# Sixteen modulation rows spread over fourteen weight blocks instead of eight, and the compression's matrices fetched at the end of the first phase

## The chip, the cores and the metric

The kernel is one program on one core of a Trainium2 chip. The metric is the device time of one execution in microseconds (us); lower is better. The engines are PE (TensorE), DVE (VectorE), ACT (ScalarE), POOL (GpSimd) and SP (SyncE, which only issues DMAs here). PE's clock is granted in two levels, 1.2 and 2.4 GHz; the profile gives it as a share of the higher one.

## The reference: what is computed

Two transformer-like blocks run one after the other on an activation of 256 tokens by 2048 features. Only the first matters here. Cut to its core:

```
mod = silu(c) @ ada_w + ada_b                      # 6 vectors of 2048: sh1, sc1, g1, sh2, sc2, g2
h = rmsnorm(x) * norm1_g * (1 + sc1) + sh1
z = h @ w_in                                       # q, kc, vc, ks, vs, kw, vw, gates, lx, ly, ga, gb
k_cmp = gelu(blocks(kc + pos_k) @ w1_k) @ w2_k     # compression of 32 tokens, stride 16: 15 keys in 4 groups
v_cmp = gelu(blocks(vc + pos_v) @ w1_v) @ w2_v
o_a = compressed + selected + window attention of q    # 16 heads in 4 groups
o_b = gelu(ly) * recurrence(conv(lx))
y = (sigmoid(ga) * (o_a @ proj_a) + sigmoid(gb) * (o_b @ proj_b)) @ w_out
x = x + g1 * y;  then a gated feed-forward block, scaled by g2
```

All is float32. The product with a weight matrix is made of three reduced-precision products: weights and activations are each split in a high and a low part.

## The kernel before: tiles, ring and order

**First phase.** For each of 16 chunks c of 128 features, DVE computes two columns of `mod` (sc1 and sh1 of this chunk), from these a chunk of `h1`, and PE multiplies it with 2048 columns of w_in (`wfour`, a ring of 3, full float32). That gives kc, vc and the first k and v. This is `first_rows`, called by `prologue`. At its end `prologue` splits the first weights of the second phase and evacuates kc and vc out of PSUM (`evac(j, 0)` and `evac(j, 1)`).

**Second phase.** The rest is a list of blocks (`Group`), each 512 output columns. A block has 4 *slots* of 1 MB of weights (128 x 2048 floats) and each slot has 2 *units* of 24 matmuls. The blocks of the first part are, in order: k1, v1, gates (one short unit), q0, q1, lx0, ly0, q2, lx1, ly1, q3, lx2, ly2, lx3, ly3, then ga, gb, pa, pb four times.

**The ring.** SP loads the slots into `wraw`, a ring of RAW = 5 places, in the order of the list `SLOTS`. The load of entry z goes to place z % 5 and waits until entry z - 5 is done: for a weight slot until PE has multiplied both its units (`pe_units`), for a modulation row until DVE has used it (`ada_done`). SP issues in order, so a load that waits holds back all behind it.

**The split.** While PE works on unit u, ACT copies the high part of unit u + 5 (LEAD) into `whi` (line 1124, 6 places) and DVE subtracts to get the low part `wlo` (line 1129). 

**Modulation rows.** A modulation row is 128 of the 12288 columns of ada_w, transposed: 1 MB, which takes one place of the ring. `ada` (line 1105) multiplies it with silu(c) and sums: one column of `mod`. The first 32 are used in the first phase. The others lie between the weight slots: `g.ada[s] = [n]` puts row n behind slot s of block g, and DVE computes it right after the low part of this slot's second unit. Rows 32 to 47 give g1, which is first read by the blocks of w_out, long after the stretch of this change.

**Jobs.** `walk` runs on every engine and interleaves with the units the steps of jobs: `compress(0)` and `compress(1)`, then attention `nsa(i)` and recurrence `lru(i)` for i = 0 to 3, at fixed unit numbers counted from the start of q1:

```python
    for make, at in ((nsa, ((0, 16), (28, 43), (51, 66), (75, 88))), (lru, ((19, 28), (43, 51), (67, 75), (88, 96)))):
```

PE's first work in nsa(i) is line 445, which waits until DVE has come through everything before it, lru(i - 1) included. Every engine executes its own list in order: if DVE waits at a `wlo` for weights that have not arrived, all its job steps behind wait too, and so does PE at its next job matmul.

**Compression's matrices.** `wcmp` holds 32 matrices of 128 x 128 (2 MB) and `w2` one more. Both are loaded by POOL's queue in `compress`: those of k when DVE signals POOL at the start of `compress(0)`, those of v into the same place when `compress(0)` is through. In POOL's list behind them is the first load of the recurrence's gate matrices (`wgate`).

Of the kernel before, what the change touches and what calls it, by code (L numbers as in the profile page):

```python
# [12 lines left out]
P = 128  # L13
T = 256
D = 2048
DC = D // P
EPS = 1e-6
NEG = -1e30
N_CMP = 15
# [33 lines left out]
def groups():  # L53
    G = Group
    out = [G("kc", 0, "w_in", 2048, 4, "h1"), G("vc", 0, "w_in", 2560, 4, "h1")]
    for i in range(2):
        out += [G("k", i, "w_in", 3072 + 1024 * i, 4, "h1"), G("v", i, "w_in", 3584 + 1024 * i, 4, "h1", "N")]
    out += [G("gates", 0, "w_in", 5120, 1, "h1", "GATES")]
    q = lambda i: G("q", i, "w_in", CB * i, 4, "h1")
    lx, ly = (lambda i: G("lx", i, "w_in", 5168 + CB * i, 4, "h1")), (lambda i: G("ly", i, "w_in", 7216 + CB * i, 4, "h1"))  # L60
    out += [q(0), q(1), lx(0), ly(0), q(2), lx(1), ly(1), q(3), lx(2), ly(2), lx(3), ly(3)]
    for i in range(4):
        out += [G("ga", i, "w_in", 9264 + CB * i, 4, "h1"), G("gb", i, "w_in", 11312 + CB * i, 4, "h1"),
                G("pa", i, "proj_a", CB * i, 4, "oa"), G("pb", i, "proj_b", CB * i, 4, "ob")]
    out += [G("wout", i, "w_out", CB * i, 4, "m1") for i in range(4)]
    for half in range(2):
        for i in range(6):
            at = half * FF // 2 + CB * i
            out += [G("gate", i, "ffn_up", at, 4, "h2", half=half), G("val", i, "ffn_up", FF + at, 4, "h2", half=half)]
        out += [G("down", i, f"ffn_down{half}", CB * i, 6, f"hid{half}", half=half) for i in range(4)]  # L70
    out += [G("u2", i, "w_in_2", 2560 + CB * i, 4, "h3") for i in range(2)]
    out += [G("kv2", 0, "w_in_2", 1024, 4, "h3", "TN")]
    out += [G("q2", i, "w_in_2", CB * i, 4, "h3") for i in range(2)]
    out += [G("ag2", i, "w_in_2", 1536 + CB * i, 4, "h3") for i in range(2)]
    out += [G("z2", i, "w_in_2", 3584 + CB * i, 4, "h3") for i in range(2)]
    out += [G("ga2", i, "w_in_2", 4608 + CB * i, 4, "h3") for i in range(4)]
    out += [G("pa2", i, "w_attn_proj_2", CB * i, 2, "at") for i in range(4)]
    out += [G("gs2", i, "w_in_2", 6656 + CB * i, 4, "h3") for i in range(4)]
    for i in range(2):
        out += [G("gluA", i, "w_glu_2", CB * i, 2, "ys"), G("gluB", i, "w_glu_2", 1024 + CB * i, 2, "ys")]  # L80
    out += [G("ps2", i, "w_ssm_proj_2", CB * i, 2, "sg") for i in range(4)]
    out += [G("wout2", i, "w_out_2", CB * i, 4, "m2") for i in range(4)]

    def of(kind, i, half=0):
        return next(n for n, g in enumerate(out) if (g.kind, g.i, g.half) == (kind, i, half))


    at = [(out[of(kind, i)], s) for kind, i in (("k", 1), ("v", 1), ("q", 0), ("q", 1), ("lx", 0), ("ly", 0), ("q", 2), ("lx", 1))
          for s in (1, 3)]
    for n, (g, s) in enumerate(at):  # L90
        g.ada[s] = [32 + n]
    at = [(out[of(kind, i)], s) for i in range(4) for kind in ("ga", "gb", "pa", "pb") for s in (1, 3)]
    for n, (g, s) in enumerate(at):
        g.ada[s] = [(64 if n % 2 == 0 else 48) + n // 2]
    at = [(out[of(kind, i)], s) for i in range(4) for kind in ("gate", "val") for s in (1, 3)]
    for n, (g, s) in enumerate(at):
        g.ada[s] = [80 + n]
    for kind, i, half in (("gate", 0, 0), ("u2", 0, 0)):
        out[of(kind, i, half)].flush = True
    return out, of  # L100


def build_program(nc, ctx, xT, vecs, cvec, W, small, turns_dram, lru_dram, outT):
    base = 16640

    def put(name, at, shape, dt=F32):
        size = 4
        for n in shape[1:]:
            size *= n
        assert base + at + size <= nc.sbuf_usable_end, name  # L110
        return nc.alloc_sbuf_tensor_at(name, list(shape), dt, offset=base + at)
# [4 lines left out]
    K = 1024  # L116


    z0, z1, z2, rM, rW = 0, 32 * K, 64 * K, 96 * K, 112 * K
# [4 lines left out]
    h1, m1 = put_pair("h1", z0, DC), put_pair("m1", z0, DC)  # L124
# [16 lines left out]
    blocks = put("blocks", z2 + 20 * K, [P, 32, 60])  # L141
    hidc = put("hidc", z2 + 28 * K, [P, 2, 64])
    kcmp = put("kcmp", z2 + 29 * K, [P, 64])
    w2 = put("w2", z2 + 29 * K + 256, [P, P])
    vcmp = put("vcmp", z2 + 30 * K, [P, 4, P])
    smB, sm0B = put("smB", z2 + 16 * K, [P, 2, T]), put("sm0B", z2 + 18 * K, [P, 2, P])
    wcmp = put("wcmp", z1, [P, 32, P])
    pct = put("pct", rM + 5 * K, [16, 4, T])
    sm = put("sm", rM + 9 * K, [P, 2, T])
    pt = put("pt", rM + 11 * K, [P, 2, 384])  # L150
# [76 lines left out]
    def sem(name):  # L227
        return ctx.enter_context(nc.semaphore(name))
# [4 lines left out]
    consts_in, c_in, consts_made = sem("consts_in"), sem("c_in"), sem("consts_made")  # L233
    x_in, four_in = [sem(f"x_in{n}") for n in range(4)], [sem(f"four_in{n}") for n in range(3)]
    c_made = sem("c_made")
    wcmp_in, wgate_in, x_back, spilled, xf_back = (sem("wcmp_in"), sem("wgate_in"), sem("x_back"),
                                                   sem("xf_spilled"), sem("xf_back"))
    turns_out, cz_in = sem("turns_out"), sem("cz_in")
    lru_out, lru_in = sem("lru_out"), sem("lru_in")
# [2 lines left out]
    S = {}  # L242
# [9 lines left out]
    at = 0  # L252
# [133 lines left out]
    def compress(j, which):  # L386
# [1 line left out]
        me = j.me  # L388
        pos, src = ("cmp_pos_k", kc4) if which == 0 else ("cmp_pos_v", vc4)
        ins = None  # L390
        yield from j.hand("to_pool", "dve", "pool", j.drained())
        if me == "pool":
            if which == 1:
                j.eng.wait_ge(S["pe_to_dve"], j.ready["cmp"][0])
            po.dma_start(wcmp[:, :, :], small["cmp_w1"][which].rearrange("l d e -> d l e")).then_inc(wcmp_in, 16)
            po.dma_start(w2[:, :], small["cmp_w2"][which]).then_inc(wcmp_in, 16)
        if me == "dve":
            j.eng.wait_ge(*evacuated("kc" if which == 0 else "vc", 0))
        for l in range(32):
# [4 lines left out]
                                 src[:, :, l:l + 225:16], V(pos, l), None, ALU.add)  # L404
        yield from j.hand("to_pe", "dve", "pe", j.drained())
        if me == "pe":
            j.eng.wait_ge(wcmp_in, 32 * (which + 1))
            for l in range(32):
                ins = te.matmul(bank[1][:, 0, 0:60], wcmp[:, l, :], blocks[:, l, :], start=(l == 0), stop=(l == 31))  # L409
        yield from j.hand("pe_to_act", "pe", "act", ins)  # L410
        if me == "act":
            ins = sc.activation(hidc[:, which, 0:60], bank[1][:, 0, 0:60], ACT.Gelu_apprx_tanh)
        yield from j.hand("act_to_pe", "act", "pe", ins)
        if me == "pe":
            if which == 0:
                ins = te.matmul(bank[2][:, 0, 0:60], w2[:, :], hidc[:, 0, 0:60], start=True, stop=True)
            else:
                for g in range(4):
                    ins = te.matmul(flat(bank[2][0:N_CMP, :, :])[:, g * P:(g + 1) * P],
                                    hidc[:, 1, g * N_CMP:(g + 1) * N_CMP], w2[:, :], start=True, stop=True)  # L420
        v = j.give("pe_to_dve", "pe", ins)
        j.ready["cmp"].append(v)
        yield
# [710 lines left out]
    def split_unit(j, u):  # L1134
        if j.me == "act":
            split_act(j.eng, u)
        if j.me == "dve":
            split_dve(j.eng, u)
# [3 lines left out]
    def prologue(j):  # L1142
# [20 lines left out]
        j.take("act_to_dve", "dve", c_ready)  # L1163
        for c in range(DC):
            first_rows(j, c)
        for u in range(U4, U4 + 4):
            split_unit(j, u)
        for g in range(2):
            for _ in evac(j, g):
                pass  # L1170
        split_unit(j, U4 + 4)

    def first_rows(j, c):
# [549 lines left out]
```

## Time and profile before

| | |
|---|---|
| time, median of 3 executions | 2901.43 us (2900.73 to 2903.86) |
| the profiled execution: time | 2896.86 us |
| its span | 2895.1 us |
| mean granted PE clock | 0.956 |
| busy: PE, DVE, ACT, POOL | 2662.9, 1864.0, 1090.7, 201.0 us |
| DMA | 568.08 MB, mean 196 GB/s |

The profiled execution took 1.8 us more than its span and lies 4.6 us under the median. Busy time is a sum over an engine's instructions. A row "A <- B" in a view of waits says that A stood idle until B ended. "DVEq" is DVE's own queue reaching a semaphore signal, and a line such as "PE bank L445" names the engine, the tile written and the line of the kernel. A row of windows has a stretch and its length in us, then the busy us and (instructions) of PE, PE's weight loads, DVE, ACT and POOL, then the granted PE clock, the busy share of the DMA engines and their GB/s. A row in order of time has start, length, engine, line, operation and tiles, and in brackets the idle time before it and what ended it.

### The profile page before, as it was taken

Reading aid. Unit: us, or ns where it says so; the run is one execution under the profiler, and the core shown is the slowest. Engines: PE = TensorE matmul, PEld = TensorE weight load, DVE = VectorE, ACT = ScalarE, POOL = GpSimd, SP = SyncE. Lnnn points to the kernel's source line nnn. Section 1 sums busy time; section 2 is a strip of 40 time slices with the busy share of each in tenths; the row PEclk is TensorE's granted clock in tenths of the full one; section 3 lists DMA queues with packets and bytes.
Section 4 is the critical chain, followed back from the end, with each engine's and each line's share of the span. In section 5 each row is a group of like instructions: output and inputs, shape, how many; then the busy total and the mean of one; then the engine's idle time right before and its main releaser. Section 6 shows DMA issues by size and latency. Waiting matters only on the chain.

```text
span 2895.1 us, 47700 instructions
## 1 busy us (share of the span) xinstructions
PE 2662.9 (92%) x20334; PEld 2562.5 (89%) x20334; DVE 1864.0 (64%) x2583; ACT 1090.7 (38%) x1350; POOL 201.0 (7%) x172
## 2 busy tenths in 40 slices
PE   6979787997999999899999999999898888889999
PEld 4778776997899999799999999999888777789999
DVE  6854555666576666578975566654558777777563
ACT  1022342553433333335443344444333443434432
POOL 0000000000000000000265520000000000000000
PEclk9978897999999999899999999999999898999999
DMA  8946352442677777377766665555464433345554
GB/s 352 425 173 213 121 196 95 160 139 95 226 271 281 277 263 255 123 276 262 242 217 208 220 214 181 188 178 171 134 204 147 131 120 125 126 157 170 176 192 145
DMA packets 237251, 568.08 MB, mean 196 GB/s; under 512 B 11216, under 2 KB 15312, under 8 KB 222576
## 3 DMA queue, kind: packets, MB, share of 16 engines
q1 hardware_dynamic: 227568, 530.31, 53.2%
q0 software_dynamic: 9472, 34.74, 3.2%
q8 instruction: 160, 2.62, 0.4%
q14 instruction: 51, 0.42, 0.0%
HBM read 550.85 MB, written 14.16 MB: 195 GB/s over the span
## 4 chain that ended last, share of the span: by engine, by line
PE 70%; DVE 13%; DVEq 5%; ACT 4%; DMA 4%; issue 2%; PEld 0%; PEldq 0%; SPq 0%; POOL 0%; ACTq 0%
PE pair L1622 60%; DVE wlo L1129 4%; DMA wraw<-w_in_dram 2%; PE pair L1201 2%; ACT whi L1124 2%; PE bank L1201 1%; PE bank L1206 1%; PE bank L409 1%; DVE wraw L1105 1%; DMA wraw<-ffn_up_dram 1%; DVEq L1021 1%; DVEq L321 1%; DVEq L847 1%; PE pair L1628 1%; PE bank L609 1%
## 5 line engine op out<-in xcount | busy, mean ns | idle before, releaser
L1129 DVE TENSOR_TENSOR wlo<-wraw,whi 128x1024 fp32r<-128x1024 f32 x777 | 964.2, 1254 | 851.2 <-ACT whi L1124 829.4
L1124 ACT ACTIVATE whi<-wraw 128x1024 fp32r<-128x1024 f32 x777 | 809.1, 1056 | 1555.8 <-PE pair L1622 927.2
L1622 PE MATMUL pair<-h_hi,whi 128*128 128x256 f32 x3936 | 1146.2, 291 | 24.8 <-DVE h_lo L331 15.6
L1622 PE MATMUL pair<-h_lo,whi 128*128 128x256 f32 x3936 | 1129.8, 287 | 0.0
L1622 PE MATMUL pair<-h_hi,wlo 128*128 128x256 f32 x3936 | 1128.6, 287 | 0.0
L1622 PEld LDWEIGHTS pair<-h_hi,whi 128*128 128x128 f32 x3936 | 773.2, 196 | 48.0 <-issue 39.8
L1622 PEld LDWEIGHTS pair<-h_lo,whi 128*128 128x128 f32 x3936 | 773.0, 196 | 0.7
L1622 PEld LDWEIGHTS pair<-h_hi,wlo 128*128 128x128 f32 x3936 | 771.8, 196 | 0.0
L1105 DVE SCALAR_TENSOR_TENSOR wraw<-wraw,cb 128x2048 f32<-128x2048 f32 x96 | 218.8, 2286 | 18.6 <-DMA wraw<-ada_wT_dram 17.9
L1622 PE MATMUL pair<-hid_hi,whi 128*128 128x256 f32 x768 | 218.5, 284 | 0.0
L1622 PE MATMUL pair<-hid_lo,whi 128*128 128x256 f32 x768 | 217.3, 283 | 0.0
L1622 PE MATMUL pair<-hid_hi,wlo 128*128 128x256 f32 x768 | 217.3, 283 | 0.0
L1622 PEld LDWEIGHTS pair<-hid_lo,whi 128*128 128x128 f32 x768 | 147.4, 192 | 0.2
L1622 PEld LDWEIGHTS pair<-hid_hi,whi 128*128 128x128 f32 x768 | 147.4, 192 | 0.2
L1622 PEld LDWEIGHTS pair<-hid_hi,wlo 128*128 128x128 f32 x768 | 147.4, 192 | 0.0
L1622 PE MATMUL pair<-m_hi,whi 128*128 128x256 f32 x512 | 145.5, 284 | 0.0
L1622 PE MATMUL pair<-m_lo,whi 128*128 128x256 f32 x512 | 144.9, 283 | 0.0
L1622 PE MATMUL pair<-m_hi,wlo 128*128 128x256 f32 x512 | 144.9, 283 | 0.0
L1622 PEld LDWEIGHTS pair<-m_lo,whi 128*128 128x128 f32 x512 | 98.3, 192 | 0.1
L1622 PEld LDWEIGHTS pair<-m_hi,whi 128*128 128x128 f32 x512 | 98.3, 192 | 0.1
L1622 PEld LDWEIGHTS pair<-m_hi,wlo 128*128 128x128 f32 x512 | 98.3, 192 | 0.0
L1622 PE MATMUL pair<-oa_hi,whi 128*128 128x256 f32 x256 | 72.8, 284 | 3.6 <-DVE wlo L1129 3.6
(416 smaller groups left out, 3321.8 us busy)
## 6 DMA issues: line engine op xcount, KB each, us to landing
wraw<-w_in_dram SPq DMA_DIRECT2D x156, 1024.0 KB, 5.2
wraw<-ada_wT_dram SPq DMA_DIRECT2D x96, 1024.0 KB, 5.4
wraw<-ffn_up_dram SPq DMA_DIRECT2D x96, 1024.0 KB, 5.1
wraw<-ffn_down_dram SPq DMA_DIRECT2D x48, 1024.0 KB, 5.1
wraw<-w_out_dram SPq DMA_DIRECT2D x32, 1024.0 KB, 5.1
wfour<-w_in_dram SPq DMA_DIRECT2D x16, 1024.0 KB, 9.3
wraw<-proj_a_dram SPq DMA_DIRECT2D x16, 1024.0 KB, 7.1
wraw<-proj_b_dram SPq DMA_DIRECT2D x16, 1024.0 KB, 6.1
```

The lines of the kernel that those rows point to most:

```text
L321: return ve.drain() if self.me == "dve" else None
L409: ins = te.matmul(bank[1][:, 0, 0:60], wcmp[:, l, :], blocks[:, l, :], start=(l == 0), stop=(l == 31))
L609: ins = te.matmul(bank[2 * a + n // 2][:, n % 2, :], wgate[:, a, n, :], t1[:, n, :], start=True, stop=True)
L847: en.drain()
L1021: ve.drain()
L1105: ve.scalar_tensor_tensor(out=wraw[:, slot, :], in0=wraw[:, slot, :], scalar=1.0, in1=cb[:, :], op0=ALU.mult, op1=ALU.mult, accum_out=mod[ ...
L1124: sc.activation(whi[:, r, 0:w], wraw[:, z % RAW, 1024 * half:1024 * half + w], ACT.Copy).then_inc(hi_ready, 1)
L1129: ve.tensor_tensor(wlo[:, z % RAW, half, 0:w], wraw[:, z % RAW, 1024 * half:1024 * half + w], whi[:, r, 0:w].bitcast(F32), ALU.subtract).t ...
L1201: ins = te.matmul(out, w[:, g * CB + o * P:g * CB + (o + 1) * P], x, start=(c == 0 and o % 2 == 0), stop=(c == DC - 1), skip_group_check=True)
L1206: ins = te.matmul(flat(bank[2 + b][:, :, :]), x[:, b * P:(b + 1) * P], w[:, 3 * CB:4 * CB], start=(c == 0), stop=(c == DC - 1))
L1622: ins = te.matmul(pair[:, o, :], w[:, at_w + o * P:at_w + (o + 1) * P], x, start=(k == 0 and o % 2 == 0 and t == 0), stop=(k == last and t ...
L1628: ins = te.matmul(flat(pair[:, 2 * b:2 * b + 2, :]), x[:, b * P:(b + 1) * P], w[:, at_w:at_w + CB], start=(k == 0 and t == 0), stop=(k == ...
```

## The change

It has two parts.

The sixteen modulation rows 32 to 47 keep their number and order but get other places: the blocks k1 and v1 keep two each (behind slots 1 and 3), and q0 to q3, lx0 to lx3 and ly0 to ly3 get one each, behind slot 1. Before, q0, q1, lx0, ly0, q2 and lx1 had two each and the later six none.

The matrices of the compression get two places each (`wcmp[0]` where it was, `wcmp[1]` on the place of `h1_f`, which is free once PE has read the last chunk and DVE has split it). POOL loads those of k when 30 of the first 32 modulation rows are used, and those of v when the first phase is through on PE. DVE no longer signals POOL in `compress`. Also, DVE evacuates kc and vc before the fourth unit's low part and not behind it; the modulation row behind this unit moves with it.

```diff
-    at = [(out[of(kind, i)], s) for kind, i in (("k", 1), ("v", 1), ("q", 0), ("q", 1), ("lx", 0), ("ly", 0), ("q", 2), ("lx", 1))
-          for s in (1, 3)]
+    at = [(out[of(kind, 1)], s) for kind in ("k", "v") for s in (1, 3)]
+    at += [(out[of("q", i)], 1) for i in range(4)] + [(out[of(kind, i)], 1) for i in range(4) for kind in ("lx", "ly")]
+    at.sort(key=lambda a: (out.index(a[0]), a[1]))
     for n, (g, s) in enumerate(at):
         g.ada[s] = [32 + n]
...
-    w2 = put("w2", z2 + 29 * K + 256, [P, P])
+    w2 = [put("w2_k", z2 + 29 * K + 256, [P, P]), put("w2_v", z2 + 28 * K + 512, [P, P])]
...
-    wcmp = put("wcmp", z1, [P, 32, P])
+    wcmp = [put(f"wcmp{n}", z1 + 16 * n * K, [P, 32, P]) for n in range(2)]
...
-        yield from j.hand("to_pool", "dve", "pool", j.drained())
-        if me == "pool":
-            if which == 1:
-                j.eng.wait_ge(S["pe_to_dve"], j.ready["cmp"][0])
-            po.dma_start(wcmp[:, :, :], small["cmp_w1"][which].rearrange("l d e -> d l e")).then_inc(wcmp_in, 16)
-            po.dma_start(w2[:, :], small["cmp_w2"][which]).then_inc(wcmp_in, 16)
+        yield
...
-            j.eng.wait_ge(wcmp_in, 32 * (which + 1))
+            j.eng.wait_ge(wcmp_in[which], 32)
...
-        for u in range(U4, U4 + 4):
+        if me == "pool":
+
+            for which in range(2):
+                if which == 0:
+                    j.eng.wait_ge(ada_done, 2 * DC - 2)
+                else:
+                    j.eng.wait_ge(pe_units, U4)
+                    j.eng.wait_ge(S["to_pe"], j.ready["h1"][-1])
+                po.dma_start(wcmp[which][:, :, :], small["cmp_w1"][which].rearrange("l d e -> d l e")).then_inc(wcmp_in[which], 16)
+                po.dma_start(w2[which][:, :], small["cmp_w2"][which]).then_inc(wcmp_in[which], 16)
+        for u in range(U4, U4 + 3):
             split_unit(j, u)
         for g in range(2):
             for _ in evac(j, g):
                 pass
+        split_unit(j, U4 + 3)
         split_unit(j, U4 + 4)
```

**SP's ring** in the stretch from q0 on. Before (L1554 is a weight slot, L1539 a modulation row), with what each load waits for:

```order
L1554 DMA wraw<-w_in_dram 128x4x512 [waits pe_units]
L1554 DMA wraw<-w_in_dram 128x4x512 [waits ada_done]
L1539 DMA wraw<-ada_wT_dram 128x2048 [waits pe_units]
L1554 DMA wraw<-w_in_dram 128x4x512 [waits pe_units]
L1554 DMA wraw<-w_in_dram 128x4x512 [waits ada_done]
L1539 DMA wraw<-ada_wT_dram 128x2048 [waits pe_units]
```

The same stretch in the changed kernel (L1561 and L1546 are the same two loads):

```order
L1546 DMA wraw<-ada_wT_dram 128x2048 [waits pe_units]
L1561 DMA wraw<-w_in_dram 128x4x512 [waits ada_done]
L1561 DMA wraw<-w_in_dram 128x4x512 [waits pe_units] x3
L1546 DMA wraw<-ada_wT_dram 128x2048 [waits ada_done]
L1561 DMA wraw<-w_in_dram 128x4x512 [waits pe_units] x4
```

One place in three held a modulation row before; now it is one in five, so that every modulation row goes to the same place of the ring and every weight slot waits for the slot four before it.

**POOL's list** where the second phase begins. Before:

```order
L395 DMA wcmp<-cmp_w_k_dram 128x32x128 [waits to_pool]
L396 DMA w_79<-cmp_w_k_dram 128x128
L395 DMA wcmp<-cmp_w_v_dram 128x32x128 [waits pe_to_dve,to_pool]
L396 DMA w_79<-cmp_w_v_dram 128x128
L688 DMA wgate<-lru_wa_dram 128x4x128
L688 DMA wgate<-lru_wi_dram 128x4x128
```

and in the changed kernel:

```order
L1170 DMA wcmp_84<-cmp_w_k_dram 128x32x128 [waits ada_done]
L1171 DMA w_k<-cmp_w_k_dram 128x128
L1170 DMA wcmp_85<-cmp_w_v_dram 128x32x128 [waits to_pe,pe_units]
L1171 DMA w_v<-cmp_w_v_dram 128x128
L684 DMA wgate<-lru_wa_dram 128x4x128
L684 DMA wgate<-lru_wi_dram 128x4x128
```

The order is the same; both waits lie earlier in the program, and the two gate loads, which have no wait of their own, move ahead with them.

**DVE's list** in nsa(2), where no modulation row was before. Here is the part of head 2 in the kernel before (L1129 is the low part, L329 and L331 put away a head's output, L525 to L533 are the softmax's weights):

```order
L514 TENSOR_SCALAR st<-st 128x4
L1129 TENSOR_TENSOR wlo<-wraw,whi 128x1024 [waits hi_ready] x2
L329 CAST oa_hi<-bank 128x256 [waits pe_to_dve]
L331 TENSOR_TENSOR oa_lo<-bank,oa_hi 128x256
L525 RECIPROCAL st<-st 128x4 [waits act_to_dve]
```

and in the changed kernel:

```order
L510 TENSOR_SCALAR st<-st 128x4
L1125 TENSOR_TENSOR wlo<-wraw,whi 128x1024 [waits hi_ready]
L1101 SCALAR_TENSOR_TENSOR wraw,mod<-wraw,cb 128x2048 [waits w_loaded2]
L1125 TENSOR_TENSOR wlo<-wraw,whi 128x1024 [waits hi_ready]
L330 CAST oa_hi<-bank 128x256 [waits pe_to_dve]
```

The modulation row stands between the low parts of two units. It does so at both its places in nsa(2) and at the one that nsa(3) gains; those in lru(1) and lru(2) stand between a low part and line 633.

## Rows read from the trace of the kernel before

**Rows 1.** The page's chain that ended last: shares of the span by engine.

```profile
PE 70%; DVE 13%; DVEq 5%; ACT 4%; DMA 4%; issue 2%; PEld 0%; PEldq 0%; SPq 0%; POOL 0%; ACTq 0%
```

**Rows 2.** Windows from one nsa's first matmul (L445) to the next one's.

```profile
290.48:439.48 149.00, 114.44 (x808) 109.15 (x808) 83.33 (x130) 58.41 (x100) 2.04 (x3) 0.87 0.43 152
439.48:557.25 117.77, 99.52 (x689) 94.47 (x689) 66.79 (x116) 51.41 (x93) 2.05 (x3) 0.88 0.40 134
557.25:657.85 100.60, 93.38 (x689) 89.68 (x689) 63.22 (x112) 51.66 (x93) 2.04 (x3) 0.94 0.43 137
```

**Rows 3.** Waits of PE, 290 to 440 us: total, times, longest.

```profile
PE bank L445 <- DVEq L321: 16.5, 2, 12.2
PE bank L565 <- DVE sm L533: 11.2, 2, 9.7
```

**Rows 4.** Waits of PE, 557 to 658 us.

```profile
PE bank L445 <- DVEq L321: 9.8, 2, 6.3
```

**Rows 5.** Waits of ACT, 180 to 760 us.

```profile
ACT whi L1124 <- DMA wraw<-w_in_dram: 153.7, 22, 17.3
```

**Rows 6.** The chain, 286 to 345 us: start, us, what.

```profile
290.48 3.60 PE bank L445 x16
294.08 7.09 PE pair L1622 x48
301.19 4.93 DMA wraw<-w_in_dram
...
334.71 2.87 PE pair L1622 x24
```

**Rows 7.** Waits of PE, 180 to 300 us.

```profile
PE bank L409 <- DVEq L321: 13.5, 1, 13.5
PE bank L445 <- DVEq L321: 4.3, 1, 4.3
PE bank L419 <- ACT hidc L412: 1.8, 1, 1.8
PE pair L1622 <- DVE v L1258: 0.7, 1, 0.7
```

**Rows 8.** The chain, 140 to 200 us.

```profile
152.85 13.25 PE pair L1622 x96
...
166.11 8.71 DMA wraw<-w_in_dram
...
185.32 13.91 PE bank L409 x64
```

**Rows 9.** Windows at the end of the first phase; columns as in Rows 2.

```profile
133.00:151.50 18.50, 16.48 (x65) 11.91 (x63) 15.39 (x21) 4.38 (x5) 0.00 (x0) 1.00 1.03 414
151.50:160.30 8.80, 7.45 (x50) 7.48 (x51) 8.43 (x11) 2.70 (x3) 0.00 (x0) 0.81 0.06 24
```

**Rows 10.** DMA issues, 120 to 260 us: KB each, us to landing.

```profile
wcmp<-cmp_w_k_dram POOLq DMA_DIRECT2D x1, 2048.0 KB, 10.5
```

**Rows 11.** DMA queues, 227 to 228 us, POOL's: packets, MB, share.

```profile
q0 software_dynamic: 65, 0.27, 68.1%
```

**Rows 12.** ACT in order of time, 143 to 162 us.

```profile
145.95 2.00 ACT L1124 ACTIVATE whi<-wraw 128x1024 fp32r<-128x1024 f32 x2 [0.55 <-DMA wraw<-w_in_dram]
```

**Rows 13.** DVE in order of time, 130 to 153 us.

```profile
131.00 2.29 DVE L1105 SCALAR_TENSOR_TENSOR wraw<-wraw,cb 128x2048 f32<-128x2048 f32 x1
...
151.53 1.22 DVE L1258 COPY kc<-pair 128x1024 f32<-128x1024 f32 x1
```

**Rows 14.** Groups of instructions, 300 to 760 us: the modulation rows on DVE.

```profile
L1105 DVE SCALAR_TENSOR_TENSOR wraw<-wraw,cb 128x2048 f32<-128x2048 f32 x10 | 22.9, 2288 | 9.6 <-DMA wraw<-ada_wT_dram 9.6
```

**Rows 15.** DVE in order of time, the low parts behind three gaps.

```profile
572.14 1.23 DVE L1129 TENSOR_TENSOR wlo<-wraw,whi 128x1024 fp32r<-128x1024 f32 x1 [3.58 <-ACT whi L1124]
...
609.30 1.23 DVE L1129 TENSOR_TENSOR wlo<-wraw,whi 128x1024 fp32r<-128x1024 f32 x1 [3.87 <-ACT whi L1124]
...
675.73 1.23 DVE L1129 TENSOR_TENSOR wlo<-wraw,whi 128x1024 fp32r<-128x1024 f32 x1 [4.02 <-ACT whi L1124]
```

More of the change, by code:

```diff
@@ L235, in build_program @@
     c_made = sem("c_made")
-    wcmp_in, wgate_in, x_back, spilled, xf_back = (sem("wcmp_in"), sem("wgate_in"), sem("x_back"),
+    wcmp_in, wgate_in, x_back, spilled, xf_back = ([sem("wcmp_k_in"), sem("wcmp_v_in")], sem("wgate_in"), sem("x_back"),
                                                    sem("xf_spilled"), sem("xf_back"))
@@ L406, in compress @@
         if me == "pe":
-            j.eng.wait_ge(wcmp_in, 32 * (which + 1))
+            j.eng.wait_ge(wcmp_in[which], 32)
             for l in range(32):
-                ins = te.matmul(bank[1][:, 0, 0:60], wcmp[:, l, :], blocks[:, l, :], start=(l == 0), stop=(l == 31))
+                ins = te.matmul(bank[1][:, 0, 0:60], wcmp[which][:, l, :], blocks[:, l, :], start=(l == 0), stop=(l == 31))
         yield from j.hand("pe_to_act", "pe", "act", ins)
@@ L415, in compress @@
             if which == 0:
-                ins = te.matmul(bank[2][:, 0, 0:60], w2[:, :], hidc[:, 0, 0:60], start=True, stop=True)
+                ins = te.matmul(bank[2][:, 0, 0:60], w2[0][:, :], hidc[:, 0, 0:60], start=True, stop=True)
             else:
@@ L419, in compress @@
                     ins = te.matmul(flat(bank[2][0:N_CMP, :, :])[:, g * P:(g + 1) * P],
-                                    hidc[:, 1, g * N_CMP:(g + 1) * N_CMP], w2[:, :], start=True, stop=True)
+                                    hidc[:, 1, g * N_CMP:(g + 1) * N_CMP], w2[1][:, :], start=True, stop=True)
         v = j.give("pe_to_dve", "pe", ins)
```

## The prediction

> **What bounds the kernel now.** I read the page's chain first: over the whole span PE carries 70% of it, with DVE and its queue 18% and DMA 4% [rows 1]. That is an average, so I went to the stretch that the change touches, cut at the first matmul of each attention job, since each piece then holds the same jobs (one nsa, one lru). The three pieces last 149.00, 117.77 and 100.60 us [rows 2]. They hold 28, 23 and 24 units (job table: 0, 28, 51, 75), and a unit alone costs PE 2.87 us (24 matmuls, [rows 6]). The third piece has no modulation row, the second has two in its first sixteen units, the first has seven. What the reader is to see in rows 2: the first piece has 4 units more than the third, some 11.5 us, but lasts 48.4 us longer, and its PE clock is 0.87 against 0.94.
>
> What ends the idle time: in 290 to 440 us PE waited 16.5 us at L445 and 11.2 us at L565, both for DVE [rows 3]. DVE itself is busy only 83.33 of 149.00 us [rows 2], so it isn't short of throughput; it is late. It is late because it stands behind a low part, which stands behind ACT, and ACT waited 153.7 us in 22 waits for weights to land [rows 5]. The chain shows the link: the load at 301.19 is on it for 4.93 us [rows 6].
>
> Why a load is on the path follows from the ring. A weight slot loads when a slot of the ring is freed; its split is due when PE begins the unit five before its own. With two slots, a modulation row, two slots, the first slot of a pair waits for the fourth unit to end, while its split is due as that same unit begins: 2.87 us before the load can even be issued. It lands 2.87 + 4.93 = 7.8 us late. With no modulation rows the load is issued 3 units (8.6 us) ahead of the split and lands in time. With one place in five for modulation, each weight slot waits for the slot four before it: it is issued one unit, 2.87 us, ahead and lands 4.93 - 2.87 = 2.1 us late, in stretches where PE does nothing but units. So the change removes most of the lateness, not all.
>
> **The change, term by term**, against the profiled execution (2896.86 us, span 2895.1).
>
> *A. Start of the second phase.* The DMA engines are full from 133 to 151.5 us (414 GB/s) and idle after (24 GB/s until 160.3) [rows 9]. The k matrices are now issued when row 30 is used, at 131.00 + 2.29 = 133.3 us [rows 13], inside the full stretch: 2.1 MB at 414 GB/s is 5.1 us, by which all weights still to come move back. The second slot's weights, split at 145.95 [rows 12], then come at 151.1. DVE's list now puts the copy of kc behind three low parts and no modulation row: ACT 1.0, low part 1.2, copy 1.2 after 151.1 gives kc free at 154.6, against 151.53 + 1.22 = 152.75 now [rows 13]. PE can begin at about 154.7 and not 152.85: 1.9 us lost. Without the 5.1 us, kc would be free near 149.5, and PE would gain 3.3 us and the slow-clock part of the first four units (13.25 us against 4 x 2.87 = 11.5): that is the other bound, 5.0 us gained. Next, the load at 166.11 took 8.71 us because the k matrices (10.5 us to landing [rows 10]) were in flight; without them it is the 4.93 of rows 6: 3.8 gained. What follows (first part of the splits, blocks, L409 at 185.32 [rows 8]) keeps its length. A = 3.8 - 1.9 = 2 us, upper bound 8.8, lower bound -1.9 (the v matrices and gates, now issued near 150, still fill the engines when this load comes; they are 2.7 MB, 6.5 us, and the engines have until 168). The 13.5 us wait at L409 [rows 7] otherwise stays.
>
> *B.* The v matrices no longer load near 217 to 232 us. The waits of 1.8 and 0.7 us [rows 7] stand behind late weights: 2.5 us.
>
> *C.* The wait of 4.3 us at nsa(0)'s L445 [rows 7] is behind a load of the last slots of q1, which now comes one unit of waiting earlier and lands before q0 ends. With it goes the slow clock after it: L445 3.60 and the next two units 7.09 us against 5.74 [rows 6]; taking half of the first, 1.8 + 1.3. C = 7.4 us.
>
> *D.* First piece: at the third's length plus 4 units it would be 100.60 + 11.5 = 112.1 us; it lasts 149.00. D = 36.9.
>
> *E.* Second piece: 100.60 - 2.9 = 97.7 against 117.77. E = 20.1.
>
> *F. What the modulation rows cost where they come to.* Each of the three pieces now has three, and nsa(3) one. One costs DVE 2.29 us [rows 14]. In the third piece the first two and the one in nsa(3) stand just ahead of low parts before which DVE is idle for 3.58, 3.87 and 4.02 us, waiting for ACT [rows 15]: hidden, with 1.3 to 1.7 us to spare. If that cover went, each would cost up to 2.29 us. The one in lru(2) falls where ACT leads. So the price is the remaining lateness of loads, 2.1 us, where nothing covers it: at the end of each recurrence, whose L445 wait of 6.3 us remains [rows 4], plus 1 us a piece for the rest, by choice. F = -3 x 3.1 = -9. Bounds: 0, and 38 (six rows moved at 2.29 = 14, and 2.0 us for each of the twelve blocks with a row).
>
> The rule of the Trainium skill for a load's length ("DMA: Bandwidth & Descriptors", Anatomy of one DMA) is about 2.0 us plus the bytes over 436 GB/s. That makes 4.4 us of 1 MB, as an estimate, where the row has 4.93; the remaining lateness would be 1.5 us and F about -7.5, so the time would come out 1.5 us lower. The row decides.
>
> Sum: 2 + 2.5 + 7.4 + 36.9 + 20.1 - 9 = 59.9 us. The profiled execution would take 2837; from the median of the runs, 2901.43, it is **2841.5 us**. Everything behind ga0 has the same ring as before and is taken as unchanged.
>
> **The rivals.**
>
> *1. Half.* The pieces do not fall to the third's length, since a load that is 2.1 us late still holds DVE in each slot and PE's clock drops after each stall. For it: the low parts are in DVE's list ahead of every job step. Against it: jobs stretch a unit to 100.60 / 24 = 4.2 us on average, which leaves 0.7 us of the 2.1. Half of D and E, 28.5 us, is missing: **2870 us**.
>
> *2. The early fetch costs the first phase itself.* POOL's queue took 68.1% of the engines in a microsecond in which it shared them with SP's loads [rows 11], so the last chunk of w_in in the first phase can come late and stall PE, which does not wait there now. Price: 5.1 us and the slow clock after it, 1.7: **2848 us**. The page named above says (Queues, rings and completion order) that an engine alternates between queues packet by packet, which speaks for this case; rows 11 agree with it.
>
> *3. Nothing.* The loads are on the chain only because they end last, and the hand-overs between ACT, DVE and PE take their place: D and E vanish, 2.9 us remain: **2898.5 us**. Against it: the third piece has the same hand-overs.
>
> *4. Slower.* One modulation row in five places is enough to keep the first two pieces late, and the third and fourth become late too. D over its seven rows is 5.3 us each; six rows come to new places: +32, less A to C, 12: **2921 us**. It decides once a load is late by more than the gaps of rows 15, 3.6 us, and not 2.1.
>
> **How the numbers follow.** The sum as worked out 0.60 (2828 to 2856), half 0.19, early fetch 0.10, nothing 0.05, slower 0.06. Low end: F at 0 and A at its upper bound give 2901.43 - 75.7 = 2826; I take 2828. High end: F at its bound, 38, gives 2870.5, as does the first rival, with 5 us beside it: 2876. What is left out is the last two cases and some of the first rival. A change of under 0.2% (5.8 us) can't be told from none here. Faster by more: 0.60 + 0.19 + 0.10 = 0.89; within 0.05; slower 0.06.
>
> **What would show it.** From one L445 to the next, 28, 23 and 24 units should take about 115, 101 and 104 us, with PE's clock above 0.92; ACT's waits for w_in should fall under a third of 153.7 us; L565's 9.7 us wait should be gone. The first L1622 should stand near 154.7 us, and the load after its fourth unit should take about 5 us. The modulation rows in nsa(2) should stand in DVE's gaps without a wait for DMA. The prediction is wrong if these pieces stay above 120 us, if PE stalls before the first phase ends, or if the third piece grows past 110.

## The result and the profile after

The changed kernel takes **2836.48 us** (median of 4 executions, 2831.71 to 2841.58), the kernel before, run beside it, 2902.64 us (median of 4, 2900.73 to 2904.44). The ratio is 0.9772, with a 95% interval of 0.9752 to 0.9792: 2.3% faster. I had said 2841.5, in a range of 2828 to 2876.

The profiled execution took 2831.71 us, its span 2829.9, with a mean PE clock of 0.965. It is the fastest of the four, 4.8 us under their median, so stretches are compared between the two profiled executions: 2895.1 to 2829.9 us, 65.2 us less.

The page's chain of the changed kernel, beside [rows 1]:

```profile
PE 72%; DVE 14%; DVEq 5%; ACT 3%; DMA 3%; issue 2%; PEldq 0%; PEld 0%; SPq 0%; POOL 0%; ACTq 0%
```

That says little. The windows from one nsa's first matmul to the next say nearly all; the columns are those of [rows 2]:

```profile
282.66:393.82 111.16, 104.11 (x811) 99.89 (x809) 74.20 (x122) 60.48 (x101) 2.05 (x3) 0.99 0.54 185
393.82:493.99 100.17, 93.04 (x688) 89.07 (x688) 68.42 (x117) 51.88 (x93) 2.05 (x3) 0.94 0.46 158
493.99:595.58 101.59, 92.24 (x689) 88.54 (x689) 69.74 (x118) 51.98 (x93) 2.05 (x3) 0.94 0.49 166
```

The pieces went from 149.00, 117.77 and 100.60 us to 111.16, 100.17 and 101.59: -37.8, -17.6 and +1.0, together -54.4. The reader can split that further. Length less PE's busy time is PE's idle time: 60.0 us in the three pieces before, 23.5 now, 36.5 less. The other 17.9 is PE's busy time itself, for the same number of matmuls: the clock in the first two pieces rose from 0.87 and 0.88 to 0.99 and 0.94. So the stalls of these pieces were paid a second time, by the slower matmuls behind them.

Waits of PE in the changed kernel, 270 to 700 us (total, times, longest):

```profile
PE bank L441 <- DVEq L322: 19.4, 3, 8.4
PE bank L561 <- DVE smB L529: 6.0, 2, 3.8
PE bank L561 <- DVE sm L529: 3.6, 4, 1.3
PE bank L493 <- DVEq L322: 2.6, 2, 1.6
```

In the same stretch of the kernel before (L445 and L565 are L441 and L561 there):

```profile
PE bank L445 <- DVEq L321: 26.2, 4, 12.2
PE bank L565 <- DVE sm L533: 18.0, 5, 9.7
PE bank L582 <- ACT pt L571: 8.4, 2, 6.9
PE bank L497 <- ACT pct L490: 7.5, 2, 4.2
```

The long wait inside the attention is gone, and those for ACT with it. What stays is the wait at the start of each nsa, as at the end of [rows 4]. ACT's waits for weights, 180 to 760 us, beside [rows 5]:

```profile
ACT whi L1120 <- DMA wraw<-w_in_dram: 98.5, 32, 11.3
```

They fell by 55 us, but there are more of them: 32 of 3.1 us on average where there were 22 of 7.0. The longest, 11.3 us, lies before nsa(0). Inside the three pieces the waits are 8 of 6.8 us, 3 of 9.7 and none before, and 10 of 2.6, 7 of 1.8 and 3 of 2.1 us in the changed kernel, none over 4.3. That is near the lateness which the prediction worked out, 7.8 and 2.1 us. The loads of the modulation rows were late as well: in the three pieces DVE waited 7.5 us in four waits for them before, and not at all now.

The chain where the second phase begins, beside [rows 8]:

```profile
130.32 21.18 DMA wraw<-w_in_dram
...
155.07 13.60 PE pair L1629 x96
...
168.69 5.25 DMA wraw<-w_in_dram
...
184.44 13.91 PE bank L405 x64
```

The first unit starts 2.2 us later than before, the load behind the fourth takes 5.25 us and not 8.71, and the compression's first matmul comes 0.9 us earlier.

### The profile page after: what moved, and what is told of

Same layout as the page of the kernel before. It is cut to its first block, busy times and chain, and to the rows that moved or that the text cites. A ratio compares the mean times of both kernels' runs of the same rounds, so it can differ in the third digit from the quotient of the medians.

```text
span 2829.9 us, 47698 instructions
## 1 busy us (share of the span) xinstructions
PE 2643.3 (93%) x20334; PEld 2546.4 (90%) x20334; DVE 1864.5 (66%) x2583; ACT 1092.6 (39%) x1350; POOL 200.1 (7%) x172
## 4 chain that ended last, share of the span: by engine, by line
PE 72%; DVE 14%; DVEq 5%; ACT 3%; DMA 3%; issue 2%; PEldq 0%; PEld 0%; SPq 0%; POOL 0%; ACTq 0%
PE pair L1629 62%; DVE wlo L1125 4%; ACT whi L1120 2%; DMA wraw<-w_in_dram 1%; PE pair L1208 1%; PE pair L1635 1%; PE bank L405 1%; PE bank L1208 1%; PE bank L1213 1%; DVE wraw L1101 1%; DVEq L1017 1%; DVEq L843 1%; PE pair L1622 1%; DVEq L322 1%; PE bank L346 1%
```

## The experiments

Each was timed beside the kernel before on the same chip. "Pieces" are the three stretches between the first matmuls of nsa(0) to nsa(3) in the profiled execution.

**Spread only**: the kernel before with nothing but the new places.

```diff
-    at = [(out[of(kind, i)], s) for kind, i in (("k", 1), ("v", 1), ("q", 0), ("q", 1), ("lx", 0), ("ly", 0), ("q", 2), ("lx", 1))
-          for s in (1, 3)]
+    at = [(out[of(kind, 1)], s) for kind in ("k", "v") for s in (1, 3)]
+    at += [(out[of("q", i)], 1) for i in range(4)] + [(out[of(kind, i)], 1) for i in range(4) for kind in ("lx", "ly")]
+    at.sort(key=lambda a: (out.index(a[0]), a[1]))
```

> The kernel before with only the sixteen modulation rows spread; the compression's matrices are fetched as before. Theory (the ring): nearly the whole gain is the spread's. From one first matmul of an attention job (L445 of the kernel before) to the next the pieces should last about 103, 100 and 102 us as in the changed kernel, against 149.0, 117.8 and 100.6, and the time be 2838 to 2843 us. Rival (the early fetch carries the first piece, because its transfers made the chain late before q1): the first piece stays above 115 us and the time above 2850 us.

Measured: 2838.9 us (2837.68 to 2841.9), ratio 0.9777 (0.9764 to 0.9791); pieces 111.87, 100.33, 102.93. The spread alone brings 64 of the 66 us. (The 103 us that I expected for the first piece "as in the changed kernel" was a slip; it has 111.16 there.) Of [rows 7], PE's waits of 1.8 us (for ACT) and of 4.3 us (at nsa(0)) are gone in this run.

**Fetch only**: the changed kernel with the old list of places.

```diff
-    at = [(out[of(kind, 1)], s) for kind in ("k", "v") for s in (1, 3)]
-    at += ...
+    at = [(out[of(kind, i)], s) for kind, i in (("k", 1), ("v", 1), ("q", 0), ("q", 1), ("lx", 0), ("ly", 0), ("q", 2), ("lx", 1))
+          for s in (1, 3)]
```

> The changed kernel with the modulation rows at their old places. Theory: the fetch alone is worth 1 to 8 us (terms A, B and part of C): 2895 to 2902 us; the pieces stay near 149, 118 and 101 us; the compression's first matmul starts near 184.4 us as in the changed kernel. Rival: below 2885 us.

Measured: 2898.69 us (2896.49 to 2903.14), ratio 0.9985 (0.9976 to 0.9994): a gain of 4 us, by the interval 2 to 7. The pieces are no shorter than before: 151.45, 119.16, 100.99. The compression's first matmul stands at 184.53 us, as expected. PE's waits of 1.8 and 4.3 us, which the spread removed, are not removed by the fetch: from the second compression's first matmul to nsa(0), where both lie, it takes 34.79 us against 34.85 before and 28.46 with the spread alone. nsa(0) starts at 289.28 us; with the spread alone at 286.53; with both at 282.66, against 290.48.

**Fetch later**: the k matrices only when the first phase is through on PE, with those of v right behind them.

```diff
                 if which == 0:
-                    j.eng.wait_ge(ada_done, 2 * DC - 2)
+                    j.eng.wait_ge(pe_units, U4)
```

> The changed kernel, but POOL waits with the matrices of k until PE is through the first phase (about 149 us), where the DMA engines fall idle. Theory of term A (the fetch of k pushes back the first weights by 5.1 us): the first unit of the second phase starts at 149.6 to 151 us instead of 155.1, the compression's first matmul at 178 to 181 instead of 184.4, the time is 4 to 6 us under the changed kernel. Rival (k and v matrices together now stand before the slot loaded after the fourth unit, so nothing is won): the compression's first matmul stays at 184 us or later.

Measured: 2834.59 us (2831.67 to 2836.65), ratio 0.976 (0.9747 to 0.9774), not to be told from the changed kernel. Its chain shows why:

```profile
148.98 11.77 PE pair L1629 x96
...
160.76 11.51 DMA wraw<-w_in_dram
```

The first unit starts 6.1 us earlier, and without the slow clock (11.77 for 13.60 us), as the bound of term A said. Then the load behind the fourth unit takes 11.51 us in place of 5.25 and eats most of it: the compression's first matmul comes at 182.77 us, 1.7 us earlier than in the changed kernel, between the theory's 178 to 181 and the rival's 184. POOL's queue (q0) and SP's (q1) in 161 to 170 us of this run (packets, MB, share):

```profile
q0 software_dynamic: 589, 2.17, 62.5%
q1 hardware_dynamic: 503, 1.33, 38.5%
```

**Fetch apart**: the same for k, and v five units later, behind that load.

```diff
                 if which == 0:
-                    j.eng.wait_ge(ada_done, 2 * DC - 2)
+                    j.eng.wait_ge(pe_units, U4)
                 else:
-                    j.eng.wait_ge(pe_units, U4)
+                    j.eng.wait_ge(pe_units, U4 + 5)
```

> The changed kernel with k's matrices fetched when PE is through the first phase and v's only when PE is through unit 5 of the second. Theory: the weights for the third slot, loaded after the fourth unit (near 161 us), no longer share the engines with v's matrices and land in about 5 us, where they took 11.5 with both fetches at 149 us and 5.25 in the changed kernel. First unit at 149 us, compression's first matmul at 177 to 179 us against 184.4, and 4 to 8 us under the changed kernel in total: 2829 to 2833. Rival: the first matmul of the compression stays above 182 us, then something else than this load holds it.

Measured: 2829.83 us (2823.52 to 2832.63), ratio 0.9744 (0.9729 to 0.9759). The load now takes 5.24 us, and both gains stand:

```profile
148.98 11.76 PE pair L1629 x96
...
160.76 5.24 DMA wraw<-w_in_dram
```

The compression starts at 176.5 and nsa(0) at 274.82 us, 7.8 us before the changed kernel. The median is 6.7 us lower, though the two ranges overlap by 0.9 us.

**Short rows, in the old places and in the new**: DVE multiplies rows 36 to 47 in 64 columns instead of 2048; loads, places and waits stay.

```diff
+        n = 64 if 36 <= col < 48 else D
-        ve.scalar_tensor_tensor(out=wraw[:, slot, :], in0=wraw[:, slot, :], scalar=1.0, in1=cb[:, :], op0=ALU.mult,
+        ve.scalar_tensor_tensor(out=wraw[:, slot, 0:n], in0=wraw[:, slot, 0:n], scalar=1.0, in1=cb[:, 0:n], op0=ALU.mult,
```

In the old places: 

> The kernel before, where the twelve modulation rows 36 to 47 are loaded and hold their places as before but DVE multiplies only their first 64 columns (part of the modulation is left out). It takes 12 x 2.2 = 26 us of DVE time out and leaves the ring alone. Theory (late loads): the pieces stay near 149 and 118 us, less 2.2 us for each row that stood on the chain, at most five: 2890 to 2900 us. Rival (DVE's time for the rows is what the spread relieves): most of D and E goes, the time is under 2860 us.

In the new places: 

> The changed kernel, where DVE multiplies only the first 64 columns of rows 36 to 47 (part of the modulation is left out); loads and places as in the changed kernel. It splits the 14 us that leaving the rows out altogether gave. Theory of term F (the rest is lateness of loads, since the rows themselves fall into DVE's gaps): at most 4 us under the changed kernel, 2832 to 2836 us. Rival (DVE's 2.29 us for a row is on the path after all, and the ring's remaining lateness costs nothing): 2821 to 2827 us, pieces near 106.8, 96.8 and 99.5.

Measured in the old places: 2888.92 us (2885.88 to 2891.02), ratio 0.9948 (0.9933 to 0.9964), pieces 146.46, 114.17, 100.48. DVE's busy time in the first piece fell by 14.3 us and the piece by 2.5. In the new places: 2835.33 us (2832.44 to 2837.29), ratio 0.9758, against 2836.48 with full rows. So DVE's time for the rows was worth 14 us at most before, and is worth about 1 us now, which can't be told from nothing. Most of the gain did not come from DVE's work moving into gaps, and what the rows still cost is not DVE's work.

**No rows**: rows 36 to 47 are neither loaded nor computed (g1 is set to zeros there, so this part of the modulation is left out); the ring holds only weights from q0 on.

```diff
     at = [(out[of(kind, 1)], s) for kind in ("k", "v") for s in (1, 3)]
-    at += ...
...
+        ve.memset(mod[:, :], 0.0)
```

> The changed kernel without the modulation rows 36 to 47 at all (part of the modulation is left out; 12 MB of loads and 12 times 2.29 us of DVE fewer). It measures term F, what the spread rows still cost. By the pieces of the changed kernel (111.2, 100.2, 101.6) against a stretch with no row (109 to 112, 97.7, 100.6) the rest is 0 to 5 us: 2831 to 2836 us. By the prediction's F it would be 9 us: 2827. Rival (DVE's time is the bound): 26 us, 2810.

Measured: 2822.31 us (2817.93 to 2825.26), ratio 0.9719 (0.9706 to 0.9732).

```profile
282.89:389.64 106.75, 103.66 (x810) 99.84 (x809) 66.49 (x115) 59.52 (x100) 2.04 (x3) 1.00 0.46 147
389.64:486.44 96.80, 92.34 (x688) 88.58 (x688) 62.04 (x111) 51.87 (x93) 2.05 (x3) 0.96 0.42 139
486.44:585.91 99.47, 92.25 (x688) 88.55 (x688) 63.34 (x112) 51.65 (x93) 2.04 (x3) 0.95 0.43 138
```

In their new places the rows cost 4.4, 3.4 and 2.1 us in the three pieces, 9.9 together in the profiled executions; by the medians of whole runs it is 14 us. Without rows ACT waits for no weight load at all in the first two pieces. Since DVE's own time is worth about 1 us, what is left is the room that the rows take in the ring or the transfer of their 12 MB; no run takes these two apart.

**Late pairs**: the changed kernel with no row from q0 to lx1, and the twelve as pairs in ly1, q3, lx2, ly2, lx3 and ly3, so that the dense stretch lies at the other end.

```diff
-    at += ...
+    at = [(out[of(kind, i)], s) for kind, i in (("k", 1), ("v", 1), ("ly", 1), ("q", 3), ("lx", 2), ("ly", 2), ("lx", 3), ("ly", 3))
+          for s in (1, 3)]
```

> The changed kernel with the twelve modulation rows of the stretch two to a block in ly1, q3, lx2, ly2, lx3 and ly3, and none in q0 to lx1: as many rows as before, in pairs again, mirrored to the later blocks. Theory (it is the density, one place of the ring in three, that makes loads late): the first piece falls to 109 to 113 us, the third, which now has six rows, rises from 101 to 120 to 135, the second lies between (105 to 115); the total comes back to 2885 to 2905 us. Rival (the blocks at the start are the sensitive ones and the later ones hide rows): the third piece stays under 108 us and the time under 2845.

Measured: 2918.19 us (2915.15 to 2921.64), ratio 1.0051 (1.0036 to 1.0065).

```profile
284.84:391.24 106.40, 103.66 (x810) 99.84 (x809) 66.50 (x115) 59.18 (x100) 2.04 (x3) 1.00 0.46 146
391.24:503.07 111.83, 92.71 (x689) 88.24 (x689) 70.94 (x119) 51.98 (x94) 2.05 (x3) 0.92 0.44 149
503.07:646.08 143.01, 102.44 (x689) 97.40 (x689) 76.77 (x124) 51.60 (x93) 2.04 (x3) 0.82 0.40 140
```

The loss moved with the pairs. The third piece went from 101.59 to 143.01 us for the same matmuls, and its clock from 0.94 to 0.82. That is more than the 120 to 135 us expected, and so is the total (2885 to 2905 expected): another 39.5 us were lost behind nsa(3) (2273.82 us against 2234.32 in the changed kernel), where the last of these pairs lie. The first piece, with 28 units and no rows, takes 106.40 us, which shows a second time that the stage itself was never slow.

**Split one unit later**: the kernel before, old places and old fetch, with LEAD 4.

```diff
-LEAD = 5
+LEAD = 4
...
-        split_unit(j, U4 + 4)
```

> The kernel before with the split four units ahead of PE and not five. No load, row or place moves; only the moment at which ACT and DVE want a slot is one unit (2.87 us) later, so a load is 4.9 us late for it and not 7.8. Theory (lateness of the load against the split holds DVE's job steps): the first two pieces shrink by a third of what the spread takes off them, 15 to 25 us together, 2878 to 2890 us. Rival (the number of rows or the transfers themselves cost): no change, 2898 to 2906, or slower because PE now waits for low parts.

Measured: 2825.17 us (2823.75 to 2825.72), ratio 0.9729 (0.9716 to 0.9743).

```profile
288.43:416.53 128.10, 112.66 (x808) 107.21 (x809) 83.19 (x130) 58.48 (x100) 2.04 (x3) 0.91 0.51 180
416.53:523.10 106.57, 97.01 (x688) 92.94 (x688) 66.35 (x116) 51.12 (x93) 2.05 (x3) 0.91 0.44 149
523.10:622.80 99.70, 92.55 (x688) 88.65 (x688) 63.08 (x112) 50.97 (x93) 2.04 (x3) 0.95 0.42 138
622.80:2822.00 2199.20, 2105.11 (x16908) 2055.51 (x16908) 1483.85 (x1928) 879.16 (x1016) 191.34 (x143) 0.98 0.58 196
```

No load is issued by another rule; the split asks for its weights 2.87 us later, and with it each row's turn on DVE comes one unit later. The pairs of rows now cost less (-20.9 and -11.2 us; the third piece, which has none, -0.9): 32 us, more than the 15 to 25 expected. ACT's waits for weights in the two are 10 of 4.4 and 2 of 4.0 us, near the 4.9 worked out. The total lies 53 us under the expected range, and most of this is in the last line, which I had not expected at all: from nsa(3) on the same stretch took 2237.25 us before. Of these 38 us, PE's waits at L1045 in the feed-forward part give 15.5 (43.2 to 27.7 us); the others were not followed one by one. This one constant is worth more than the whole change.

**Single rows behind slot 3** instead of slot 1, the rest as in the changed kernel: one place in five all the same.

```diff
-    at += [(out[of("q", i)], 1) for i in range(4)] + [(out[of(kind, i)], 1) for i in range(4) for kind in ("lx", "ly")]
+    at += [(out[of("q", i)], 3) for i in range(4)] + [(out[of(kind, i)], 3) for i in range(4) for kind in ("lx", "ly")]
```

> The changed kernel with the twelve single rows behind slot 3 of their blocks and not behind slot 1. The ring keeps its period of five, but on DVE each row moves four units on, to other gaps and in lru(0) onto the tail. Theory (density decides, DVE's gaps hide a row): 2832 to 2842 us, pieces within 3 us of 111.2, 100.2 and 101.6. Rival (the place of a row in DVE's list decides what it costs): a piece grows by 5 us or more and the time passes 2846 us.

Measured: 2870.86 us (2868.88 to 2874.35), ratio 0.9884 (0.9871 to 0.9898); pieces 115.87, 108.77, 108.87. That is 34 us over the changed kernel, so the theory that only the distance between rows counts fell, at least inside the pieces, which grew by 20.6 us. The other 17 us lie behind nsa(3) (2251.32 against 2234.32 us), and there the distance does change: the row behind ly3's last slot is followed two slots later by ga0's first, so that one place in three is a row from ly3 on and not from ga0 on. ACT's waits for the weights there (w_in, in the 164 us behind nsa(3)'s first matmul) are 28.4 us with one of 20.9, against 11.4 with 7.6. DVE in order of time in lru(0) of this run:

```profile
351.96 1.23 DVE L1125 TENSOR_TENSOR wlo<-wraw,whi 128x1024 fp32r<-128x1024 f32 x1 [1.65 <-ACT whi L1120]
353.11 2.29 DVE L1101 SCALAR_TENSOR_TENSOR wraw<-wraw,cb 128x2048 f32<-128x2048 f32 x1
355.32 0.08 DVE L1101 DVE_READ_ACCUMULATOR wraw<-wraw,cb 128x1 f32 x1
355.32 5.10 DVE L693 SCALAR_TENSOR_TENSOR t<-pair,vec,t 128x255 f32<-128x255 f32 x12
```

and of the changed kernel:

```profile
351.71 1.23 DVE L1125 TENSOR_TENSOR wlo<-wraw,whi 128x1024 fp32r<-128x1024 f32 x1 [1.65 <-ACT whi L1120]
352.85 5.10 DVE L693 SCALAR_TENSOR_TENSOR t<-pair,vec,t 128x255 f32<-128x255 f32 x12
...
368.10 2.28 DVE L1101 SCALAR_TENSOR_TENSOR wraw<-wraw,cb 128x2048 f32<-128x2048 f32 x1
370.31 0.08 DVE L1101 DVE_READ_ACCUMULATOR wraw<-wraw,cb 128x1 f32 x1
```

Behind slot 3 the row stands right ahead of the convolution (L693), whose result PE needs at L605; behind slot 1 it stands between two low parts. In the three pieces PE waits 6.1 us in 3 waits at L605, one of about 2 us in each recurrence, and never there in the changed kernel; and it waits 27.6 us at L441 for 19.4. With 3.5 us more of PE's busy time at a lower clock that is most of the 20.6. Whether DVE's time for the row causes it, short rows behind slot 3 would have shown; this was not tried, and the cause of the 20.6 us stays open.

**The best of both**: fetch apart, with LEAD 4 and with LEAD 3.

```diff
-LEAD = 5
+LEAD = 4
...
-        split_unit(j, U4 + 4)
```

(for LEAD 3 the split of U4 + 3 goes as well).

LEAD 4: 

> The kernel with the two fetches apart, and the split four units ahead instead of five. Theory: loads are now 4.93 us against an issue two units (5.7 us) ahead and are never late, so that the pieces come near those without rows (106.8, 96.8, 99.5), 5 to 9 us less than 111.3, 99.5 and 103.2; and the stages behind the attention gain as they did when the kernel before got the same setting (38 us after the last attention's first matmul). Together 2783 to 2797 us. Rival (the two cures overlap: where the spread has cured the first stage the setting gives nothing, and the later gain was part of the same repair): above 2815 us.

LEAD 3: 

> The same with the split three units (8.6 us) ahead. Lateness of loads can give nothing more in the stretch with spread rows. What can be lost: ACT and DVE need 2.3 us for a unit's parts and their longest job steps are 5.1 us (the convolution), so PE begins to wait for low parts in the dense stages. Theory: within 8 us of the one with four, more likely slower; the waits of PE for low parts rise above 20 us in total. Rival (every unit of lead costs): another 20 us or more faster.

Measured with LEAD 4: **2772.41 us** (2771.48 to 2777.09), ratio 0.9547 (0.9534 to 0.9561), 64 us under the changed kernel and below what was expected. With LEAD 3: 2801.08 us (2800.73 to 2804.54), ratio 0.9646 (0.9632 to 0.9659), 29 us more than with LEAD 4, where 8 had been expected. The first two pieces with LEAD 4:

```profile
270.98:374.29 103.31, 103.14 (x810) 99.72 (x808) 73.11 (x121) 57.15 (x99) 2.05 (x3) 1.00 0.54 186
374.29:468.14 93.85, 89.48 (x688) 85.53 (x689) 68.48 (x117) 52.58 (x95) 2.05 (x3) 1.00 0.52 181
```

In the first, PE is busy 103.14 of 103.31 us at full clock: no idle time is left to take there. The third takes 102.36 us and not the 99.5 expected. Both lines lie under the same pieces without any row at LEAD 5 (106.75 and 96.80), so the setting gives some 3 us a piece that are not the rows' lateness, and no run tells what they are; nor are the loads never late, since ACT still waits 18.7 us for them in these two pieces. Behind nsa(3) it gives 37 us (2199.30 against 2236.21). With LEAD 3 the pieces are 107.96, 103.81 and 104.97. Over the whole execution PE waits 18.0 us in 10 waits for `wlo` (7.5 in 5 with LEAD 4), but only 0.2 us of them in the pieces, so a late split doesn't explain the 17 us that these lost; that stays open. 4 is the best of the three values.

## Why the prediction was right, step by step

**The mechanism.** That a load was late against its split because modulation rows crowded the ring is shown by runs from three sides, and by ACT's waits, of 7 to 10 us each with two rows a block and of 2 to 3 us with one. Moving the rows alone carries the gain (spread only); moving them to the other end moves the loss there (late pairs); and leaving them where they are but asking later for the weights takes back 32 us of the same two pieces (LEAD 4), of which some 6 may be the setting's own (see the best of both). That it was DVE's work is excluded as more than a small part by the short rows. A ring of six places, which would have tested the lateness without moving a row or the split, was not tried.

**A, B and C** (11.9 us): the first unit came at 155.07 us, as worked out (154.7), and the load behind it took 5.25 us for the 4.93 assumed. But the four units took 13.60 us, 0.4 more than before, and only 0.9 us of A's 2 was left at the compression's first matmul. Up to the second compression's first matmul (255.6 us before, 254.2 now) another 0.5 us were gained, which is B's wait of 0.7. B's other wait, 1.8 us, lies behind this matmul, together with the 4.3 us of C; between there and nsa(0) 6.4 us were gained. B charged the 1.8 us to the fetch of the v matrices. That was wrong: it stays in fetch only and is gone in spread only, so the ring was its cause, as it was C's. By nsa(0), 7.8 us were gained in all, for 8.8 in A, B and the first part of C. The 1.8 and 1.3 us of C for the slow clock at L445 and behind it belong to the piece that L445 begins. They came (L441 takes 1.85 us now for 3.60), but they are part of what D measured.

**D and E** (36.9 and 20.1 us) **with F** (-9): together 48, and 51.1 with C's 3.1; measured 54.4. The step that was off is D's yardstick. I took the third piece's length plus four units, 112.1 us, for a first piece without rows. Without rows it takes 106.75 (no rows): the third piece has 0.94 of the clock and PE idle for 7 us, which the first need not have. D should have been 42.3, C's 3.1 included. E (97.7 assumed, 96.80 measured) and F (9 assumed, 9.9 measured) were right in size. That F is not DVE's time is shown; that it is the remaining lateness is likely, by ACT's waits of about 2 us, but its 1 us a piece "by choice" had no row behind it, so that the size of F was in part luck. The two rows in nsa(2) are hidden as worked out: behind each, DVE still waits 1.4 and 1.5 us for ACT. The total came out close also because D, too small by 5.4 us, stood against C's 3.1 us counted beside it.

**The load's length.** The prediction set a load of SP's queue beside the rule of the Trainium skill ("DMA: Bandwidth & Descriptors", Anatomy of one DMA). The page gives this rule, 2.0 us plus the bytes over 436 GB/s, as measured for loads that POOL issues, so it was the rule of another path. Here the rows decide: 4.93 us, and 5.24 and 5.25 us in the runs.

**Behind nsa(3)** the text counted on nothing; the profiled executions differ by 2.9 us there (2237.25 to 2234.32), which may be the spread of runs: it is 2236.12 to 2238.54 us in the four other runs with the same places of the rows and LEAD 5.

**The signs.** The pieces (111.16, 100.17 and 101.59 for 115, 101 and 104), the clock (0.99, 0.94, 0.94 for over 0.92), the 9.7 us wait at L565 and the rows of nsa(2) without a wait for DMA came as said. One did not: ACT's waits for weights fell from 153.7 to 98.5 us, not under a third. My own arithmetic had each load still 2.1 us late, which for the 48 slots of the twelve blocks is 101 us, so a third could not have been right; the sum of ACT's waits is a poor measure of how much PE loses.

**The rivals.** Half (2870) is refuted by the pieces: ACT's waits of about 2 us leave PE's clock at 0.94 or more and cost 10 us and not 28.5. That the slot 3 run comes out at 2870.86 is a coincidence of numbers; half of its loss lies behind nsa(3). The early fetch did not cost the first phase: PE stalls there once, for 0.34 us. Its price stands where A put it, at the start of the second phase, and fetch apart shows what it was (the first unit 6.1 us later). Nothing (2898.5) and slower (2921) are refuted by spread only; the late pairs, at 2918.19, show what the fourth rival feared, but for two rows a block and not one.

## What to carry to other kernels

When an engine waits for a transfer that has bandwidth to spare, write down for one buffer when its place comes free and when its content is asked for. What the load's length exceeds this time by is how late it is, and it can be mended at either end (spacing out the foreign tenants of the ring, or asking one unit later). Look at the constant that sets the asking first; here it was worth 77 us against the change's 66; with both, and the fetches apart, the kernel took 132 us less than the one before, run beside it (2904.52). Take a stage's floor from a run without the suspected cost, not from its neighbour, and when a placement is moved, look at the spacing at both of its ends.

## What the runs showed of the hardware

Two DMA queues need not share evenly; the one that starts first can have all for a while. In the kernel before, in the microsecond from 168 us, SP's 1 MB load had been issued 1.9 us earlier, but only POOL's queue shows packets:

```profile
q0 software_dynamic: 90, 0.37, 101.6%
```

The same load with the engines to itself (fetch apart, issued at 160.76 us) shows 177 packets and 0.36 MB in the microsecond that begins 1.9 us behind its issue, so it is not merely the start of a load that is seen here. What held SP's packets back, the trace doesn't show.

The same 1 MB load of weights took 4.93 and 5.24 us with the engines to itself, 8.71 us beside one set of matrices and 11.51 us beside two. The Trainium skill ("DMA: Bandwidth & Descriptors", Queues, rings and completion order) has an engine alternate between queues packet by packet; where both show packets in the fetch-later run the trace agrees: 35 packets of POOL's to 33 of SP's in the microsecond from 161 us, 67 to 68 in that from 166 us. The share then goes by the size of a packet: 34.3% to 66.3% in the first, where SP loads a modulation row (0.14 MB to 0.27), and 64.9% to 37.7% in the second, where it loads weights (0.25 MB to 0.14). The microsecond above doesn't agree.

The time of one and the same program spreads by some microseconds from execution to execution: the changed kernel's over 9.9 us in four (2831.71 to 2841.58), the kernel before over 3.7 in the four beside it and over 10.0 in fifteen beside the first experiments (2898.99 to 2909.01).
